# A fused mixer and expert kernel: expert stage in plain fp32 on two 64-column tiles, with a ring of six 2 MB weight pieces

## What is computed

```
grp    = argmax(softmax(xt @ rg_w + rg_b))          # 1 of 4 groups
q, e   = top_k(softmax((xt @ re_w + re_b) of grp), 2) # 2 of its 8 experts
h      = silu(xt[rows of e] @ w_gate[e]) * (xt[rows of e] @ w_up[e])
out    = sum over the 2 experts of gate * (h @ w_down[e])
```

## Time and profile before

| | us |
|---|---|
| device time, median of 3 runs | 1637.29 (1633.11 to 1638.04) |
| span of the profiled execution | 1632.2 |
| PE busy | 1494.6 (92%) |
| DVE busy | 1302.7 (80%) |
| ACT busy | 1047.0 (64%) |
| DMA | 480.04 MB, mean 294 GB/s |

### The profile page before, as it was taken

One profiled execution on the slowest core, in us unless ns is written; L12 is line 12 of the kernel. 1 busy time (PEld: TensorE's weight loads), 2 busy tenths in 40 slices (PEclk: granted clock), 3 DMA queues, 4 the chain that ended last, 5 costly groups with the idle time before them and its releaser, 6 DMA issues.

```text
span 1632.2 us, 21079 instructions
## 1 busy us (share of the span) xinstructions
PE 1494.6 (92%) x7346; PEld 1243.4 (76%) x7346; DVE 1302.7 (80%) x1029; ACT 1047.0 (64%) x786; POOL 65.4 (4%) x58
## 2 busy tenths in 40 slices
PE   6999999898689999999999999999999999999991
PEld 6999999786567777777777777777777777777771
DVE  5467786544689899988888888988889898899884
ACT  5433444544267777777777777777777777777762
POOL 1000000000000100000000000000100000010001
PEclk9999999999799999999999999999999999999996
DMA  7554545362169999999999999999999999999974
GB/s 271 184 174 155 186 160 183 128 207 90 52 262 354 365 363 349 359 353 357 354 346 373 346 350 347 352 368 351 372 346 362 349 351 360 351 379 350 355 292 159
DMA packets 90803, 480.04 MB, mean 294 GB/s; under 512 B 8815, under 2 KB 8815, under 8 KB 40212
## 3 DMA queue, kind: packets, MB, share of 16 engines
q1 hardware_dynamic: 88660, 471.23, 78.2%
q0 software_dynamic: 2112, 8.39, 1.4%
HBM read 473.29 MB, written 10.49 MB: 296 GB/s over the span
## 4 chain that ended last, share of the span: by engine, by line
PE 49%; DVE 20%; DMA 15%; ACT 8%; issue 6%; DVEq 1%; ACTq 0%; POOLq 0%; SPq 0%; POOL 0%
PE bank L1221 45%; DVE w_lo L322 14%; DMA stage<-in_w_down 9%; DMA stage<-in_w_up 5%; ACT w_hi L316 5%; DVE y_rows L1065 2%; ACT h_hi L645 1%; DVE hidden L1053 1%; PE bank L1200 1%; DMA stage<-y_sorted,slot_i 1%; PE bank L1376 1%; PE bank L1363 1%; PE bank L1364 1%; DVE h_lo L1048 0%; DMA x_tok<-in_x 0%
## 5 line engine op out<-in xcount | busy, mean ns | idle before, releaser
L322 DVE TENSOR_TENSOR w_lo<-stage,w_hi 128x2048 fp32r<-128x2048 f32 x444 | 1011.5, 2289 | 229.5 <-ACT w_hi L316 227.9
L316 ACT ACTIVATE w_hi<-stage 128x2048 fp32r<-128x2048 f32 x444 | 848.4, 1917 | 400.5 <-PE bank L1221 258.3
L1221 PE MATMUL bank<-w_hi,h_hi 128*128 128x512 f32 x1600 | 639.7, 400 | 57.3 <-DVE w_lo L322 47.7
L1221 PE MATMUL bank<-w_lo,h_hi 128*128 128x512 f32 x1600 | 625.3, 391 | 0.0
L1221 PE MATMUL bank<-w_hi,h_lo 128*128 128x512 f32 x1600 | 625.2, 391 | 0.0
L1221 PEld LDWEIGHTS bank<-w_hi,h_hi 128*128 128x128 f32 x1600 | 301.3, 188 | 158.1 <-DVE w_lo L322 88.8
L1221 PEld LDWEIGHTS bank<-w_hi,h_lo 128*128 128x128 f32 x1600 | 301.2, 188 | 65.2
L1221 PEld LDWEIGHTS bank<-w_lo,h_hi 128*128 128x128 f32 x1600 | 301.7, 189 | 58.1
L1221 PE MATMUL bank<-h_hi,w_hi 128*128 128x256 f32 x576 | 163.3, 283 | 1.5 <-DVE w_lo L322 1.5
L1221 PE MATMUL bank<-h_lo,w_hi 128*128 128x256 f32 x576 | 163.0, 283 | 0.0
L1221 PE MATMUL bank<-h_hi,w_lo 128*128 128x256 f32 x576 | 163.0, 283 | 0.0
(11 more groups left out here) (221 smaller groups left out, 584.3 us busy)
## 6 DMA issues: line engine op xcount, KB each, us to landing
stage<-in_w_gate SPq DMA_DIRECT2D x128, 1024.0 KB, 6.8
stage<-in_w_up SPq DMA_DIRECT2D x128, 1024.0 KB, 6.2
stage<-in_w_down SPq DMA_DIRECT2D x128, 1024.0 KB, 6.8
stage<-in_w_in SPq DMA_DIRECT2D x44, 1024.0 KB, 4.9
stage<-in_w_out SPq DMA_DIRECT2D x16, 1024.0 KB, 5.1
x_tok<-in_x SPq DMA_DIRECT2D x2, 1024.0 KB, 5.9
out<-x_tok SPq DMA_DIRECT2D x4, 512.0 KB, 2.7
final_w<-in_final_g SPq DMA_DIRECT2D x1, 1024.0 KB, 7.7
```

The lines of the kernel that those rows point to most:

```text
L316: nc.scalar.activation(w_hi[(br + m) % PARTS][:, :], stage[m][:, :], ACT.Copy).then_inc(hi_made, 1)
L322: nc.vector.tensor_tensor(w_lo[i][:, :], stage[m][:, :], w_hi[i][:, :].bitcast(F32), ALU.subtract).then_inc(lo_made, 1)
L1221: ins = M.matmul(dst, stationary, moving, start=start and i == 0, stop=stop and i == 2)
```

## The change

Nothing before the sorting is computed in another way. In the expert stage the weights are no longer split: they land in a ring of six buffers of 2 MB, one expert in all (gate and up by halves, then down by halves), and TensorE multiplies them in plain fp32 from there. The stationary side is a window of 64 rows. Gate goes to the lower 64 partitions of bank 0 and up to the upper 64; of down, the left 1024 result columns go to the lower and the right 1024 to the upper partitions of banks 4 and 5. One expert is done from gate to down before the next begins. Experts with over 64 rows are done again in a loop of 7 passes, entered only if there are any; the tables for it are made ahead of the first expert. The ring lies in the memory of `h_hi`, `h_lo`, `stage`, `w_hi` and `w_lo`; the first expert's six pieces are loaded as these fall free. Rows are stored as half rows with 128 indices. The diff, cut to its core (lines that are only "..." mark what is left out):

```diff
-OVER = 3
-ROWS_ACT, ROWS_DVE = 2, 2
-FEW = 32
+W_ROWS = 64
+OVER = SLOTS // W_ROWS - 1
+HD = D // 2
...
-
-OVER_BLOCK0 = MOE_BLOCK0 + 3 * E
+PIECES = 6
+PIECE = C * NB // 2
...
         x_tok = sb("x_tok", [P, T, D])
-        stage = [sb(f"stage{m}", [P, CW]) for m in range(STAGES)]
-        w_hi = [sb(f"w_hi{i}", [P, CW], F32R) for i in range(PARTS)]
-        w_lo = [sb(f"w_lo{i}", [P, CW], F32R) for i in range(PARTS)]
-        h_hi = sb("h_hi", [P, C * S], F32R)
-        h_lo = sb("h_lo", [P, C * S], F32R)
...
+        with ExitStack() as early:
+            h_hi = early.enter_context(nc.sbuf_tensor("h_hi", [P, C * S], F32R))
+            h_lo = early.enter_context(nc.sbuf_tensor("h_lo", [P, C * S], F32R))
+            stage = [early.enter_context(nc.sbuf_tensor(f"stage{m}", [P, CW], F32)) for m in range(STAGES)]
+            w_hi = [early.enter_context(nc.sbuf_tensor(f"w_hi{i}", [P, CW], F32R)) for i in range(PARTS)]
+            w_lo = [early.enter_context(nc.sbuf_tensor(f"w_lo{i}", [P, CW], F32R)) for i in range(PARTS)]
+        ring = [sb(f"ring{k}", [P, PIECE]) for k in range(PIECES)]
+        spare = sb("spare", [P, 2 * CW])
...
-        win_hi, win_lo = (z[:, 0:C * P].rearrange("p (c n) -> p c n", c=C) for z in (h_hi, h_lo))
-        hiddenT_hi, hiddenT_lo = (z[:, C * P:C * P + NB] for z in (h_hi, h_lo))
-        pick = h_hi[:, C * P + NB:C * P + NB + T * SLOTS].rearrange("p (t n) -> p t n", t=T)
+        win = spare[:, 0:C * W_ROWS].rearrange("p (c n) -> p c n", c=C)
+        hiddenT = spare[:, C * W_ROWS:C * W_ROWS + J * W_ROWS]
...
-        y_rows = sb("y_rows", [P, D])
+        y_rows = sb("y_rows", [P, HD])
         silu_g = sb("silu_g", [P, NB])
-        hidden = sb("hidden", [P, NB])
+        hidden = sb("hidden", [W_ROWS, NB])
...
         def x_sorted_from(first):
-            return zone_u[:, bass.ds(first, C * SLOTS)].rearrange("p (c n) -> p c n", c=C)[:, :, 0:P]
...
+            return zone_u[:, bass.ds(first, C * SLOTS)].rearrange("p (c n) -> p c n", c=C)[:, :, 0:W_ROWS]
...
+        def gathered_rows(k, t):
+            return ring[k][:, t * D:(t + 1) * D]
...
+            def load_piece(k, src):
+                sp.dma_start(ring[k][:, :], src).then_inc(piece_loaded[k], 16)
+
+            first_pieces = expert_pieces(0)
             for b in range(D // NB):
                 load(sp, OUT_BLOCK0 + b, columns(w_out, b * NB))
-
-            load(sp, MOE_BLOCK0, expert(0, 0))
-            load(sp, MOE_BLOCK0 + 1, expert(1, 0))
+                if b == 1:
+
+                    sp.wait_ge(used, chunk(4 * OUT_BLOCK0 - 1))
+                    load_piece(0, first_pieces[0])
+                    load_piece(1, first_pieces[1])
+
+            sp.wait_ge(lo_made, chunk(4 * MOE_BLOCK0 - 1))
+            load_piece(2, first_pieces[2])
+            load_piece(3, first_pieces[3])
+            sp.wait_ge(used, chunk(4 * MOE_BLOCK0 - 1))
+            load_piece(4, first_pieces[4])
+            load_piece(5, first_pieces[5])
 
             sp.wait_ge(sorted_done, C)
             sp.dma_start(final_w[:, :], a["final_g"].rearrange("(o d) -> o d", o=1).broadcast_to([P, D])).then_inc(fg_loaded, 16)
+
+            def load_expert(t, e):
+
+                for k, src in enumerate(expert_pieces(e)):
+                    if k in (0, 2):
+                        sp.wait_ge(in_used, 2 * t + (k // 2 - 1))
+                    if k >= 4:
+                        sp.wait_ge(down_used, 2 * t + (k - 5))
+                    load_piece(k, src)
+
             with sp.Fori(1, E) as e:
-                load(sp, g_block(e), expert(0, e))
-                load(sp, g_block(e) + 1, expert(1, e))
-                load(sp, g_block(e) + 2, expert(2, e - 1))
-            load(sp, g_block(E), expert(2, E - 1))
+                load_expert(e, e)
...
-                pool.wait_ge(y_act, ROWS_ACT * t + 2 * ROWS_ACT)
-                pool.wait_ge(y_dve, ROWS_DVE * t + 2 * ROWS_DVE)
+                pool.wait_ge(y_act, t + 2)
+                pool.wait_ge(y_dve, t + 2)
                 pool.wait_ge(row_ready, t + 1)
                 pool.sem_inc(store_started, 1)
-                count = pool.value_load(count_i[0:1, bass.ds(t, 1)], min_val=0, max_val=S)
-
-                for rows, has_these in ((FEW, count <= FEW), (P, count > FEW)):
-                    with pool.If(has_these):
-                        pool.indirect_dma_start(
-                            out=y_sorted, out_offset=bass.IndirectOffsetOnAxis(ap=row_now[0:rows, 0:1], axis=0),
-                            in_=y_rows[0:rows, :], in_offset=None, bounds_check=SLOTS - 1,
-                            oob_is_err=False).then_inc(y_stored, 16)
+                pool.indirect_dma_start(
+                    out=halves, out_offset=bass.IndirectOffsetOnAxis(ap=row_now[:, 0:1], axis=0),
+                    in_=y_rows[:, :], in_offset=None, bounds_check=2 * SLOTS - 1,
+                    oob_is_err=False).then_inc(y_stored, 16)
                 pool.wait_ge(y_stored, 16 * t + 16)
                 pool.sem_inc(rows_free, 1)
...
-            for m in range(PARTS):
-                split_hi(act, MOE_BLOCK0, MOE_BLOCK0 % 3, m)
-
...
-            def first_window(m):
-
-                act.wait_ge(sorted_act, (m + 1) * CM // 2)
-                act.wait_ge(sorted_dve, (m + 1) * CM // 2)
-                nc.scalar.activation(win_hi[:, m * CM:(m + 1) * CM, :], x_sorted[:, m * CM:(m + 1) * CM, 0:P],
-                                     ACT.Copy).then_inc(first_hi, 1)
...
+                nc.scalar.activation(win, x_sorted_from(first), ACT.Copy).then_inc(win_ready, 1)
+
+            def expert_act(t):
+
+                act.wait_ge(in_used, 2 * t + 2)
+                nc.scalar.activation(silu_g[UPPER, :], bank[0][0:W_ROWS, :], ACT.Silu).then_inc(silu_done, 1)
+                window(t + 1)
+                act.wait_ge(down_used, 2 * t + 2)
                 act.wait_ge(rows_free, t + 1)
...
+                nc.scalar.activation(y_rows[:, 0:NB], bank[4][:, :], ACT.Copy).then_inc(y_act, 1)
+
+            act.sem_inc(y_act, 1)
...
-            rows_out(E - 1, g_block(E))
+            act.wait_ge(sorted_act, C // 2)
+            act.wait_ge(sorted_dve, C // 2)
+            window(0)
+            expert_act(0)
+            act.wait_ge(tables_ready, 1)
+            with act.Fori(1, E) as e:
+                expert_act(e)
...
-            for m in range(PARTS):
-                split_lo(dve, MOE_BLOCK0, MOE_BLOCK0 % 3, m)
-
...
+            link(V.tensor_scalar(ROW_H, iota_p[:, 0:1], float(W_ROWS), None, ALU.is_ge))
+            link(V.scalar_tensor_tensor(ROW_Q, ROW_H, -float(W_ROWS), iota_p[:, 0:1], ALU.mult, ALU.add))
+            link(V.scalar_tensor_tensor(ROW_2, ROW_Q, 2.0, ROW_H, ALU.mult, ALU.add))
...
+            def row_table(at):
+
+                link(V.tensor_scalar(row_of[:, at], counts[:, at], ROW_Q, float(8 * SLOTS), ALU.is_le, ALU.mult))
+                link(V.scalar_tensor_tensor(row_of[:, at], starts[:, at], 2.0, row_of[:, at], ALU.mult, ALU.add))
+                link(V.tensor_scalar(row_i[:, at], row_of[:, at], ROW_2, None, ALU.add))
+
+            def crowded_tables():
+
+                left, start, mask, now = (over[:, i, :] for i in range(4))
+                V.tensor_copy(left, counts[:, 0:E])
+                link(V.tensor_copy(start, starts[:, 0:E]))
+                for i in range(OVER):
+                    link(V.scalar_tensor_tensor(mask, left, float(W_ROWS), ramp[:, :], ALU.is_gt, ALU.mult))
+                    link(V.tensor_reduce(KOV[:, i:i + 1], mask, AX.X, ALU.max))
+                    link(V.tensor_scalar(mask, ramp[:, :], KOV[:, i:i + 1], None, ALU.is_equal))
+                    V.scalar_tensor_tensor(start, mask, float(W_ROWS), start, ALU.mult, ALU.add)
+                    link(V.scalar_tensor_tensor(left, mask, -float(W_ROWS), left, ALU.mult, ALU.add))
+                    link(V.tensor_tensor(now, mask, start, ALU.mult))
+                    link(V.tensor_reduce(starts[:, E + i:E + i + 1], now, AX.X, ALU.add))
+                    link(V.tensor_tensor(now, mask, left, ALU.mult))
+                    link(V.tensor_reduce(counts[:, E + i:E + i + 1], now, AX.X, ALU.add))
+                row_table(slice(E, E + OVER))
...
+            def expert_dve(t):
+
+                dve.wait_ge(silu_done, t + 1)
+                V.tensor_tensor(hidden[:, :], silu_g[UPPER, :], bank[0][UPPER, :], ALU.mult).then_inc(hidden_ready, 1)
+                dve.wait_ge(hidden_turned, t + 1)
+                V.tensor_copy(hiddenT, bank[2][:, 0:J * W_ROWS]).then_inc(hiddenT_ready, 1)
+                dve.wait_ge(rows_free, t + 1)
+                V.tensor_copy(row_now[:, :], row_i[:, bass.ds(t, 1)]).then_inc(row_ready, 1)
+                dve.wait_ge(down_used, 2 * t + 2)
+                V.tensor_copy(y_rows[:, NB:HD], bank[5][:, :]).then_inc(y_dve, 1)
+
+            dve.sem_inc(y_dve, 1)
+            row_table(slice(0, E))
+            crowded_tables()
+            with dve.Fori(0, E) as e:
```

(62 more changed lines are left out.)

236 lines of the change are left out of this document (25 added, 211 removed).

## The result

The changed kernel takes **1431.68 us** (median of 4 runs, 1429.86 to 1433.32) against 1635.2 us for the kernel before in the same measurements (4 runs): ratio 0.8751, 95% interval 0.8728 to 0.8775. Forecast was 1534.4, range 1440 to 1605. The direction and the mechanism came as forecast; the gain is twice what I said, and the time lies 8 us under the range.

What follows compares the result with a forecast made beforehand. Before, TensorE and DMA were both pressed; after, transfers bound it: stream start 453.4 plus 1037.6 us at 380 GB/s to 1491.0, rows copied 1495.7, end 33.6, span 1529.3, plus 5.1: 1534.4 us; range 1440 to 1605.

Steps and rivals of the forecast that it cites:

- What bounds the kernel now: Expert stage before: TensorE 32.4 us an expert, VectorE splits 27.5, whole expert 35.3; two resources pressed at once.
- TensorE's cost of an expert: Expert stage, plain fp32: 23.9 us an expert if the two 64-column tiles overlap, 44 us without.
- rival 2: Expert stage: the tiles don't overlap, TensorE is the bound at 44.0 us an expert, 1893 us; chance 0.15.
- The transfers: Expert stage: with overlap the DMA engines become the bound, at 380 GB/s, between bounds of 357 and 419.
- my upper bound, 419 from 406 to 412: DMA rate in the kernel before with nearly idle engines: 419 GB/s, never held over 20 us; would give 1438 us.
- Rival 1: Expert stage: the DMA rate was the true limit already; at 357 GB/s 1601 us, still faster; chance 0.12.
- The sum: Whole kernel: stream from 453.4 to 1491.0 at 380 GB/s, last rows copied 1495.7, span 1529.3, time 1534.4 us.
- T+28 and T+22: Ring timing after the second piece lands at T: down ends near T+28, a next pair lands at T+22.
- rival 3: Expert stage: waits for transfers lower TensorE's clock; at 1.2 GHz throughout about 1920 us, expected only to eat slack; chance 0.04.
- The start of the stage: Before the first expert: early pieces cost 0, crowded tables' 18 us on VectorE cost 0, TensorE starts at 445.8.
- Rival 4: Expert stage: partial tile overlap, 1.25 to 1.29, TensorE at 35.2 to 36.2 us an expert, 1611 to 1643 us; chance 0.03.
- Rival 5: Expert stage: any expert with over 64 rows starts seven more passes, +232 us; given no chance.

Runs made afterwards that it cites:

- The square: Kernel before, expert stage: one matmul instead of three per product, 1611.2 us; splits of 8 columns instead of 2048, 1555.3 us; both together, 1467.1 us.
- half pieces: Changed kernel with only the first half (1 MB) of each piece loaded from the second expert on: 1248.9 us.

## Why the prediction was right or wrong

**What bounds the kernel now: wrong in one point, and it is the costly one.** "Everything stands between 27 and 35 us" had the transfers in the balance at 33 to 35. The square shows TensorE at 32.8, the splits' path with its waits for landings at 34.8, the transfers alone at 30.1.

**TensorE's cost of an expert: right.** 23.9 us, measured at 23.9. The overlap, taken from no row, holds; rival 2 is refuted for this order. The Trainium skill's 2x for 64 columns ("TensorEngine Tiling (Array Packing)", Performance Considerations) agrees with this trace: 16 records of each tile in a half start 0.43 us apart in both tiles. The 1.59x worked out from three tiles does not.

**The transfers: the step that failed is "The rate at full share ... their mean is 374 GB/s ... I take 380".** I chose the 12 stretches of 20 us with a share of 0.99 or more and took them for saturated engines; the long row's 357/0.96 = 372 seemed to agree. The runs put 426 in its place, and 418 for the old buffers and DMAs once splits and products were gone.

A high share does not mean engines at full rate, for a long packet counts as busy time for its whole length. The trace had it in its DMA records: of the 8 KB packets of the stage before, the median takes 309 ns (16 engines x 8192 bytes / 309 ns = 424 GB/s) and the mean 351. The long packets make the difference, and their share follows the rate through the runs (8 KB packets from 500 to 1160 us; the queue is the mean number of 1 MB loads between issue and landing):

| run | loads in the queue | packets over 450 ns | GB/s |
|---|---|---|---|
| 1 MB DMAs, 1 in the queue | 1.0 | 12.1% | 223 |
| kernel before | 2.2 | 8.9% | 355 |
| kernel before, one product | 2.2 | 7.7% | 362 |
| kernel before, splits of 8 columns | 2.7 | 5.1% | 384 |
| 1 MB DMAs, 2 in the queue | 2.0 | 3.3% | 386 |
| kernel before, one product and splits of 8 columns | 3.7 | 0.9% | 418 |
| 1 MB DMAs, 3 in the queue | 3.0 | 0.6% | 417 |

The changed kernel had three to five 2 MB DMAs in the queue; the prediction's "always two or more" held. Its 16 KB packets have a median of 613 ns, a mean of 616, and 0.2% over 900. With one DMA in the queue the long packets are one in eight, 763 ns on average, and nine in ten of them start 0.5 to 1.5 us after an issue. A 1 MB DMA is 128 packets, eight for each engine, so this fits the first packets of engines that had run empty. With half pieces, where the queue runs empty too, median and mean are 309 and 350. Why such a packet takes long no run shows. How many of the long packets in the kernel before are of this kind is open as well, since the trace does not name a packet's engine.

The sentence "the slow stretches at full share are not a matter of depth" is not settled by this. The mean number in the queue does not order them, 2.1 in the best stretch (880 to 900 us, 394 GB/s) and 2.4 in the worst (780 to 800, 345); the share of packets over 450 ns does, 5.4% and 10.9%.

The row that had it right was my upper bound, 419 from 406 to 412. Only 1.0% of its packets take over 450 ns. The prediction calls the engines nearly idle there, but only TensorE was: VectorE and ScalarE were busy for 4.69 and 4.44 of the 6 us, VectorE with its last split until 408.4. It had 1.9 loads in the queue on average, no more than elsewhere in this kernel, so the number in the queue would not have shown it. I set it aside as "never held over 20 us" where I should have asked what was different in it.

The Trainium skill, "DMA: Bandwidth & Descriptors", Specifications, gives about 358 GB/s of HBM per core. The same page, section Bandwidth, says that this is for both cores of a pair streaming, and measures 425 for one core with the other idle. For this kernel on one core the trace agrees with the second figure, with 426 held for over 900 us, and not with the first, which the prediction names. Rival 1 rested on the same quotient of rate and share as my forecast, and fell with it.

**The sum, term by term.** The rate is worth 394.3 / 0.380 - 394.3 / 0.426 = 1037.6 - 925.6 = -112.0 us. The start came at 450.67 instead of 445.8, +4.9: 3.4 of it lie before the router. There the last addition to x_tok (line 925 before) comes at 388.0 to 390.4 in the kernel before and the three built from it, and at 388.5 to 391.4 in the changed kernel and the nine built from that; so most of it varies by run. The means are 389.0 and 390.5: up to 1.5 us may be the early pieces', which I had put at 0. The rest is the window's start, 0.93 us of waiting and address load before its 1.06. The end took +10.5: I let the last half of down follow the last landing in 4.7 us, against my own T+28 and T+22, but TensorE was still behind with gate and up. The chain at the end:

```profile
1380.49 0.81 PE bank L1226
...
1389.31 0.60 ACT silu_g L638
1389.93 0.70 DVE hidden L994
1390.77 0.68 PE bank L1233 x4
1391.47 0.44 DVE spare L996
1391.95 7.11 PE bank L1246 x32
1399.08 0.70 DVE y_rows L1000
```

From the copy to the end 32.2 us against 33.6, -1.4; and the median stands 0.4 above the span instead of 5.1, -4.7. Together: 1534.4 - 112.0 + 4.9 + 10.5 - 1.4 - 4.7 = 1431.7.

**The clock, rival 3: the mechanism was right and nearly harmless, as forecast.** The granted clock is 0.93 in the stage on the mean. It falls where TensorE waits for a landing: after the last such wait, of 3.3 us, it is 0.50 from 1382 to 1384 us, the level of 1.2 GHz, and 0.95 in the next 2 us. This last one is on the chain: the first six records of each tile from 1380.49 on stand 0.60 to 0.86 us apart instead of 0.43, and the half takes 8.8 us instead of 6.9. That the earlier ones cost nothing is argued from the 1.01 of the DMA share, not measured by a run. With one product the mean clock was 0.60, and splits and landings set the time.

**The start of the stage:** tables and pieces cost nothing, as said. **Rival 4**, partial overlap, falls with the 23.9 us. **Rival 5**, the crowded passes, did not come: w_gate was loaded 64 times, 32 experts of two halves.

## What to carry to other kernels

A high DMA share is no proof that the transfers are the bound: compare the mean time of a packet with the median (351 and 309 ns here, 616 and 613 after), and look at what is different in the best few us of the trace, before you price a stream at the mean. When two suspects are near each other, take away both, alone and together: here the products alone gave 18 us and the splits alone 71, both together 162. And a small stationary side in plain fp32 on two tiles costs less than three split products on the whole array, if neighbours in the program address different tiles.

## What the runs showed of the hardware that I had not expected

- The DMA engines held 426 GB/s on one core over 900 us, and 427 beside VectorE and ScalarE at 83% and 71%.
- With 1 MB DMAs, each issued when an earlier one had landed: 223 GB/s with one in the queue, 386 with two, 417 with three; but 1.9 on average gave 419 for 6 us in the kernel before.
- With one 1 MB DMA in the queue one 8 KB packet in eight takes 763 ns and the others 311, and the busy share counts both alike. It fits the first packet of each engine that had run empty.
- Matmuls on two column tiles don't start strictly in program order: three records of the second tile began ahead of the last of the first. The Trainium skill, "TensorE: Matmul & The Clock Gate", Part 3, says that they do; this trace does not agree.
- Plain fp32 on two 64-column tiles reaches twice the rate of one, two streams of 512 columns in 0.43 us a record.
